# Running the two paired expert steps of a mixture-of-experts stage last instead of fifth and sixth

## The reference

```
g_prob = softmax(t @ w_group + b_group);  g_p, g_idx = top_k(g_prob, 1)
e_prob = softmax(the four expert logits of group g_idx)
e_p, e_idx = top_k(e_prob, 2)
weights = g_p * e_p / sum(e_p)
for e in range(16):
    hid = silu(t @ w_gate[e]) * (t @ w_up[e])
    out = out + combine[:, e] * (hid @ w_down[e])
x = x + out
```

## Time and profile before

| | |
|---|---|
| median of 3 runs | 1187.67 us (1186.32 to 1187.78) |
| profiled execution | 1186.32 us, span 1184.5 us |
| PE / DVE / ACT busy | 1154.2 (97%) / 790.9 (67%) / 624.1 (53%) us |
| critical chain by engine | PE 80%, DVE 9%, ACT 6%, issue 4% |
| weights moved | 222.47 MB on SP's queue, mean over the span 194 GB/s |

### The profile page before, as it was taken

One profiled execution on the slowest core, in us unless ns is written; L12 is line 12 of the kernel. 1 busy time (PEld: TensorE's weight loads), 2 busy tenths in 40 slices (PEclk: granted clock), 3 DMA queues, 4 the chain that ended last, 5 costly groups with the idle time before them and its releaser, 6 DMA issues.

```text
span 1184.5 us, 18040 instructions
## 1 busy us (share of the span) xinstructions
PE 1154.2 (97%) x7484; PEld 996.5 (84%) x7484; DVE 790.9 (67%) x914; ACT 624.1 (53%) x775; POOL 120.6 (10%) x137
## 2 busy tenths in 40 slices
PE   7999999997999999999999999999999899999998
PEld 6978997986788865578778779998999898999897
DVE  6997677646654422588898788487667955755544
ACT  5855233543544311467775556588778644534442
POOL 0100000000000000000000200067704410000000
PEclk9999999998999999999999999899999999999999
DMA  7444334511855569999891476222345455555552
GB/s 287 174 139 145 108 107 142 186 36 58 350 183 184 199 212 392 408 421 387 336 370 69 147 245 227 99 98 99 102 134 173 129 170 192 178 195 183 209 178 106
DMA packets 35151, 229.75 MB, mean 194 GB/s; under 512 B 3856, under 2 KB 6416, under 8 KB 10368
## 3 DMA queue, kind: packets, MB, share of 16 engines
q1 hardware_dynamic: 31344, 222.47, 52.0%
q10 hardware_dynamic: 3728, 6.15, 1.5%
HBM read 227.53 MB, written 1.08 MB: 193 GB/s over the span
## 4 chain that ended last, share of the span: by engine, by line
PE 80%; DVE 9%; ACT 6%; issue 4%; POOL 1%; DMA 0%; DVEq 0%; ACTq 0%
PE bank L496 21%; PE bank L498 21%; PE bank L497 20%; DVE r L1906 3%; ACT r L1328 3%; PE bank L906 2%; PE bank L506 2%; PE bank L960 1%; PE bank L668 1%; PE bank L1192 1%; POOL f L2819 1%; PE bank L861 1%; PE bank L918 1%; PE bank L783 1%; PE bank L764 1%
## 5 line engine op out<-in xcount | busy, mean ns | idle before, releaser
L496 PE MATMUL bank<-r,r 128*128 128x512 f32 (+5 forms) x1848 | 610.1, 330 | 13.6 <-DVE r L1906 8.5
L498 PE MATMUL bank<-r,r 128*128 128x512 f32 (+5 forms) x1848 | 599.3, 324 | 0.0
L497 PE MATMUL bank<-r,r 128*128 128x512 f32 (+5 forms) x1848 | 598.1, 324 | 0.0
L1906 DVE TENSOR_TENSOR r<-f,r 128x2048 fp32r<-128x2048 f32 (+3 forms) x191 | 430.6, 2262 | 161.0 <-ACT r L1328 160.7
L1328 ACT ACTIVATE r<-f 128x2048 fp32r<-128x2048 f32 (+3 forms) x191 | 358.8, 1883 | 178.4 <-PE bank L498 145.6
L496 PEld LDWEIGHTS bank<-r,r 128*128 128x128 f32 (+4 forms) x1848 | 342.2, 185 | 56.9 <-issue 17.8
L497 PEld LDWEIGHTS bank<-r,r 128*128 128x128 f32 (+4 forms) x1848 | 342.4, 185 | 31.6 <-issue 1.0
L498 PEld LDWEIGHTS bank<-r,r 128*128 128x128 f32 (+4 forms) x1848 | 342.4, 185 | 31.2
L1915 DVE TENSOR_TENSOR r<-f,r 128x512 fp32r<-128x512 f32 (+3 forms) x67 | 48.8, 744 | 30.7 <-ACT r L1872 11.2
L2819 POOL TENSOR_SCALAR f<-f,f 128x128 f32<-128x128 f32 (+1 forms) x64 | 64.2, 1019 | 44.3 <-DVE f L2603 44.3
L2782 POOL TENSOR_SCALAR f<-f 128x1 f32<-128x1 f32 x2 | 0.6, 291 | 364.0 <-ACT f L1339 364.0
(11 more groups left out here) (338 smaller groups left out, 1030.9 us busy)
## 6 DMA issues: line engine op xcount, KB each, us to landing
f<-in_weights SPq DMA_DIRECT2D x192, 1024.0 KB, 4.9
f<-in_weights SPq DMA_DIRECT2D x12, 896.0 KB, 4.7
f<-in_weights SPq DMA_DIRECT2D x8, 672.0 KB, 4.6
f<-in_weights SPq DMA_DIRECT2D x4, 882.0 KB, 5.7
f<-bias_table ACTq DMA_DIRECT2D x1, 2048.0 KB, 13.2
f<-in_mem ACTq DMA_DIRECT2D x1, 1024.0 KB, 4.9
out<-f ACTq DMA_DIRECT2D x3, 256.0 KB, 2.0
f<-in_x SPq DMA_DIRECT2D x1, 512.0 KB, 4.9
```

Of the source, the lines that this page charges most:

```text
L496: e.matmul(o, lh.r, rh.r, start=start, stop=False)
L497: e.matmul(o, lh.r, rl.r, start=False, stop=False)
L498: return e.matmul(o, ll.r, rh.r, start=False, stop=stop)
L1906: e.tensor_tensor(slot_of(n).r, slot_of(n).f, high_of(n).r.bitcast(F32), ALU.subtract).then_inc(s["w_lo"], 1)
```

## The change

The paired steps become steps 12 and 13. The places are then worked through in order of size: 0 (steps 0 to 3), 1 (4 to 7), 2 (8 to 11), 3 (12 and 13); the pair tile is now tile 4 and its slots are the last 128. Scatters move to steps 5, 6, 9 and 13 (from 5, 6, 7 and 11). The number of matmuls, units, splits and bytes is the same. The numbers in the names of units now follow the steps, so that units 24 to 31 of each kind are the paired ones (8 to 15 before).

```diff
-PAIRED = (4, 5)
-LAST_STEP = {0: 3, 1: 3, 2: 5, 3: 9, 4: 13}
-SCATTERED_IN = {5: 0, 6: 1, 7: 2, 11: 3}
-TURNED_IN = {2: 2, 4: 3, 8: 4}
-SLOTS_OF = (slice(0, 128), slice(128, 256), slice(512, 640), slice(256, 384), slice(384, 512))
+PAIRS = 12
+LAST_STEP = {0: 3, 1: 3, 2: 7, 3: 11, 4: 13}
+SCATTERED_IN = {5: 0, 6: 1, 9: 2, 13: 3}
+TURNED_IN = {2: 2, 6: 3, 10: 4}
@@ parts_of
-    return [(x + 4, 2 if x in PAIRED else 3 + (x - 6) // 4)]
+    return [(x + 4, 2 + (x - 4) // 4)]
@@ units_of
-    if x < 4:
-        return [((name, 2 * x + u), 0, x, u) for u in range(2)]
-    if x in PAIRED:
-        return [((name, 8 + 4 * (x - 4) + 2 * u + a), 3, 2 * (x - 4) + a, u) for u in range(2) for a in range(2)]
-    return [((name, 16 + 2 * (x - 6) + u), 1 + (x - 6) // 4, (x - 6) % 4, u) for u in range(2)]
+    if x < PAIRS:
+        return [((name, 2 * x + u), x // 4, x % 4, u) for u in range(2)]
+    return [((name, 2 * PAIRS + 4 * (x - PAIRS) + 2 * u + a), 3, 2 * (x - PAIRS) + a, u) for u in range(2) for a in range(2)]
@@ build
-        split.append(not (key in SOURCE and 8 <= key[1] < 16))
+        split.append(not (key in SOURCE and key[1] >= 2 * PAIRS))
@@ PE: tile_in, turn_hidden, tile_out (x not in PAIRED becomes x < PAIRS)
-                    freed[b] = ("ht_h", y + 1) if x in PAIRED else ("ht_l", hidden_lows(y))
+                    freed[b] = ("ht_l", y + 1) if x < PAIRS else ("ht_h", y + 1)
...
-                    if x in (0, 4, 6, 10):
+                    if x % 4 == 0:
...
-                                                 start=x == 4 and k == 0, stop=x == LAST_STEP[t] and k == 3, skip_group_check=True)
+                                                 start=x == PAIRS and k == 0, stop=x == LAST_STEP[t] and k == 3, skip_group_check=True)
@@ ACT: the loop over steps
-                    if x_ == STEPS - 1 and u == 1:
+                    if x_ == STEPS - 1 and key == units_of("down", x_ - 1)[2][0]:
                         hidden_high(x_)
@@ DVE: the loop over steps
-                if x == STEPS - 1:
-                    hidden_low(x)
```

More of the change, by code:

```diff
@@ L39, in parts_of @@
         return [(2 * x, 0), (2 * x + 1, 1)]
-    return [(x + 4, 2 if x in PAIRED else 3 + (x - 6) // 4)]
-def hidden_lows(y):
-    return y + 1 if y < 8 else y - 1
+    return [(x + 4, 2 + (x - 4) // 4)]
 PARTS = STEPS + 4
@@ L186, in build @@
         number.append(sum(split))
-        split.append(not (key in SOURCE and 8 <= key[1] < 16))
+        split.append(not (key in SOURCE and key[1] >= 2 * PAIRS))
     split_unit = [n for n in range(len(plan)) if split[n]]
     slots, before = [], []
-    extra = range(at["gate", 0], at["down", 31] + 1)
+    extra = range(at["gate", 0], at["down", 2 * PAIRS + 7] + 1)
     last = {}
@@ L880, in tile_in @@
                 bs = [in_bank((name, y), evac, READ_AT[read, y]) for y, _ in parts]
-                if x not in PAIRED:
+                if x < PAIRS:
                     for key, _, _, u in units_of(name, x):
@@ L889, in tile_in @@
                             for kk in range(4):
-                                k, sl = 4 * u + kk, SLOTS_OF[t]
+                                k, sl = 4 * u + kk, slice(128 * t, 128 * t + 128)
                                 m = mm3(banks[b][:, :], XGH[:, k, sl], XGL[:, k, sl], wh[:, kk, :], wl[:, kk, :], k == 0, k == 7)
@@ L924, in tile_out @@
                 for y, t in parts:
-                    if x in (0, 4, 6, 10):
+                    if x % 4 == 0:
                         for a in range(2):
                             in_bank(("dn", t, a), "y_l", 2 * t + a + 1)
-                    if x not in PAIRED:
-                        e.wait_ge(s["ht_l"], hidden_lows(y))
+                    if x < PAIRS:
+                        e.wait_ge(s["ht_l"], y + 1)
                     else:
@@ L943, in tile_out @@
                                     m = mm3(banks[bank_at["dn", t, a]][:, :], HTH[y % 2][:, k, :], HT_[y % 2][:, k, :], wh[:, kk, f], wl[:, kk, f],
-                                            x in (0, 6, 10) and k == 0, x == LAST_STEP[t] and k == 3)
+                                            x % 4 == 0 and k == 0, x == LAST_STEP[t] and k == 3)
                                 if x == LAST_STEP[t] and u == 1 and not (a == 1 and last_of_all):
@@ L969, in turn_tile @@
             def turn_tile(t):
-                sl = SLOTS_OF[t]
+                sl = slice(128 * t, 128 * t + 128)
                 b = take(("pt", t))
@@ L1552, in hidden_high @@
                         wait_unit(units_of("down", step_of(y - 2))[-1][0])
-                    dst = HT_[y % 2].f if x in PAIRED else HTH[y % 2].r
+                    dst = HTH[y % 2].r if x < PAIRS else HT_[y % 2].f
                     e.activation(dst, banks[bank_at["th", y]][:, :].rearrange("p (c s) -> p c s", c=4), ACT.Copy).then_inc(s["ht_h"], 1)
@@ L2355, in turned @@
                 e.tensor_copy(PTR[t % 4].r, banks[b][:, 0:256].rearrange("p (i t) -> p i t", i=2))
-                if t == 2:
+                if t == 4:
                     for half in range(2):
@@ L2371, in hidden @@
                         e.wait_ge(s["pe_done"], full["th", y - 2])
-                    expert = units_of("up", x)[0][2]
-                    weight = CWP[:, x - 4:x - 3] if x in PAIRED else CW[t][:, expert:expert + 1]
+                    weight = CW[t][:, x % 4:x % 4 + 1] if x < PAIRS else CWP[:, x - PAIRS:x - PAIRS + 1]
                     read_out(("hid", y), e.scalar_tensor_tensor(out=HD[y % 2], in0=banks[bank_at["up", y]][:, :], scalar=weight, in1=HG[y % 2],
@@ L2377, in hidden_low @@
             def hidden_low(x):
-                for y, _ in () if x in PAIRED else parts_of(x):
+                for y, _ in parts_of(x) if x < PAIRS else ():
                     e.wait_ge(s["ht_h"], y + 1)
```

## The result

The changed kernel takes 1195.41 us (median of 4 runs, 1193.82 to 1197.07), the kernel before 1187.31 in the same comparison: ratio 1.0074, with a 95% interval of 1.0061 to 1.0085. The forecast was 1195.2, +7.5 us; measured is +8.1. The profiled execution of the changed kernel has 1195.14 us and a span of 1193.3, which is 8.8 us more span than before.

What follows compares the result with a forecast made beforehand. PE was taken to bound the stage from end to end, with late loads delaying its end after the change. 6.5 - 0.4 + 1.4 = +7.5 us on 1187.67 gave 1195.2 us; forecast's own range 1191.8 to 1197.2, overall 1190 to 1199.

Steps and rivals of the forecast that it cites:

- The loads at the end: Steps 12 and 13: late down and `kcvc` units delay ACT's copy of tile 4's result, 6.5 us (4.5 with no lag).
- T: Start of gate(12), from which the ledger of the stage's end counts; put at about 586.6 us.
- The lag of 2.0 us: Real landings come 2.0 us later than reckoned, taken from the paired steps of before; bounds 0 and 2.0.
- From there loads never pause: From the second unit of down(11), at T + 8.2, units land every 2.49 us, as slots come free faster than they fill.
- The -0.4 us at the scatter of tile 3: Scatter moves into paired step 13, without splits ahead on DVE; 0.39 us of PE idle time in 580:603 should go.
- PE's waits: PE waits 2.3 us for loads in down(13), then 4.9 us before the final scatter.
- The clock: Behind PE's idle time at the stage's end the granted clock falls: +1.4 us, bounds 0 and 3.4.
- rival 3: Loads are slower at the end, 372 GB/s: +13.5 us, 1201; by the 358 GB/s limit some 8 us later still; chance 0.08.
- The splits put into steps 4 and 5: Splits moved from the last two steps into steps 4 and 5 cost nothing, some tenths if that cover were gone.
- sign of being wrong: Wrong if ACT's `kcvc` splits find units landed, PE waits already in up(13), or a two-tile or single-tile step lengthens.
- No load kept up (1): Rival: loads keep up, `kcvc` 1 on chip by about T + 48.5; 1187.67 - 0.4, no change; chance 0.10.
- no end got shorter (2): Rival: the end gets shorter without splits in steps 12 and 13, at most 2.0 us, 1185.7 to 1186.5; chance 0.05.

Runs made afterwards that it cites:

- e2_half_loads: Changed kernel with each unit of the paired steps loaded by half and the half used twice, so other values are computed: 0.9995 of the kernel before.
- e1_result_first: Changed kernel with ACT and DVE bringing out tile 4's result before they split `kcvc`: 1.0062 of the kernel before.
- e5_last_8_slots: Changed kernel with eight landing slots instead of nine in the expert stage: 1.0096 of the kernel before.
- e4_busy_wait: Changed kernel with 18 matmuls, their result dropped, filling PE's wait before the last scatter: 1.0068 of the kernel before.
- e0_again: Changed kernel once more, unedited: 1.0079 of the kernel before.
- e11_early_ksvs_sooner: Kernel before, with the split of `ksvs` 0 moved forward on ACT and DVE, ahead of work on the next block's norm: 0.9968, 1185.06 us.
- e3_add_early: Changed kernel with DVE adding a scatter's first two quarters before the last split of the up units, not behind it: 1.0038 of the kernel before.
- e7_pairs_middle: Kernel before with the paired steps as steps 8 and 9: 1.0042 of the kernel before.
- e8_middle_add_early: Kernel before with the paired steps as 8 and 9 and DVE's first two scatter additions ahead of its last split: 1.0018 of the kernel before.
- e6_early_8_slots: Kernel before with eight landing slots instead of nine: 1.0033 of the kernel before.

## Why the prediction was right, and where two terms were off

- **The loads at the end, right.** The prediction had 6.5 - 0.4 = 6.1 us up to the copy; it is 5.3. The rate of 421 GB/s held (423). The last expert matmuls start at T + 49.7 (forecast T + 50.0), `kcvc` 1 is split from T + 54.5 (T + 55.0), the copy is at T + 56.35 (T + 56.9). The lag of 2.0 us carried over from the earlier trace rows was about 0.5 too long. The landings in the trace say what it is made of: the second unit of down(11) lands at T + 9.1 instead of T + 8.2, and the loads do pause once, with 3.13 us instead of 2.49 between two units at 618.7 and 621.8. "From there loads never pause" was nearly right; why that unit is late is open.
- **The -0.4 us at the scatter of tile 3, misread, of the right size.** Of the 0.39 us of idle time in 580 to 603 only 0.13 is at the scatter; 0.26 is PE's wait for a weight split at 597.36. Both are gone with the splits. gate(12) starts at 589.65, where 586.6 and the two delays ahead of it (1.42 and 2.24) make 590.26, so PE gained 0.6 us ahead of the tail.
- **PE's waits, right in place and size.** For loads 1.5 us (forecast 2.3), before the last scatter 4.5 (4.9). `e2_half_loads` takes both away, `e1_result_first` the second, and `e5_last_8_slots` makes both longer.
- **The clock, right.** Forecast +1.4 with bounds 0 and 3.4; 1.6 in the profile, shown by `e4_busy_wait`. The size within the bounds was a choice, so that it came so near is partly luck. It fell as the row at 288 of the earlier trace rows had it after an idle time of 3.24 us, and as the rule of the Trainium skill ("TensorE: Matmul & The Clock Gate", "HAM oscillation — how this bites in real kernels") has it. But the stretch of low clock later in the kernel was shorter than before and gave 1.6 us back in this execution. Such stretches differ from one execution to the next (`e0_again`, `e2_half_loads` and `e11_early_ksvs_sooner` have one more near 950), and so a term of this size can't be checked in the total.
- **The figure of 358 GB/s.** Of rival 3 nothing came: 40 us at 423 GB/s, so the limit for a core that the Trainium skill names ("DMA: Bandwidth & Descriptors", "Specifications") did not bind this kernel on one core.
- **The splits put into steps 4 and 5, wrong.** "Nothing, and if that cover were gone some tenths" was 2.24 us. I compared DVE's busy time in dense steps and took steps 6 and 7 of before as the pattern for 5 and 6 now. What differs is which banks the next result takes. In step 6 of before none is taken, in step 7 two that the scatter had not used; in step 5 the second is a bank of the scatter itself, and PE waits for an addition that had no split ahead of it before. The prediction's own sign of being wrong, that a single-tile step has become longer, came true here. `e3_add_early` and `e7_pairs_middle` show it from both sides. The row to read would have been the order on DVE between the scatter and the first down product that takes its bank.
- **The total.** +8.1 us measured in the medians. The tail, which is most of it, was foreseen in its mechanism and size. That the total stands within 0.6 us of the forecast owes something to luck: 2.24 us were missing, and 0.8 too many in the tail, 1.8 given back later and a start 1.4 later stand beside them in the profiled execution.
- **The rivals.** No load kept up (1), no end got shorter (2), the loads weren't slower (3). The range of the forecast itself, 1191.8 to 1197.2, held the time.

## What to carry to other kernels

In this kernel a burst that draws on a ring of landing slots was hidden only where slow steps ahead of it had filled the ring and slower steps followed. Price such a move by counting units at the rate of the densest stretch, and look at what is queued behind the last of them on each engine. When work is put into a step, look not only at its busy time but at every bank and buffer that someone waits to see freed behind it. Before moving large work, look for the copy or addition that stands behind a late split; here such small moves in the order won back about what the placement of the pairs had cost.

## What the runs showed of the hardware that I had not expected

- A wait for a bank that another engine has to free appeared as "issue" (2.24 us at 474.68): the profile names no releaser for it. The order of work on DVE shows it, and it went with that order in `e3_add_early` and `e8_middle_add_early`.
- The loads gave 422 to 424 GB/s in dense stretches beside a PE that was busy nearly all the time: 423 over 600 to 640 here, 422 over 540 to 564 in `e7_pairs_middle`. Units of 1 MB that came in a row landed 2.46 to 2.50 us apart there, with few exceptions. A load share near 1 doesn't show such a stretch by itself: 0.98 stands beside 363 GB/s over 505 to 540 here.
- After 4.5 us of idle time the granted clock was 0.58 over 648 to 652, most of it at the lower level of 1.2 GHz, and it cost 1.6 us; the stretch at 762 to 769 was about twice as long with no idle time ahead.
- The length of a wait alone didn't tell whether the clock falls. It fell behind waits of 2.28 (`e8_middle_add_early`), 2.48 (`e7_pairs_middle`), 2.94 (`e6_early_8_slots`) and 3.51 us (`e1_result_first`), and stayed at 1.00 behind one of 2.62 us (`e6_early_8_slots`, at 488) and behind the 2.2 to 2.3 us in step 5 of seven profiles.
